# Four down projections of a fused four-layer model as seven products of half blocks in place of eight, with three weight sums on VectorE and one on GpSimd

## The reference, cut to what matters

```python
def swiglu(h, w_gate_up, w_down):
    g, u = jnp.split(h @ w_gate_up, 2, axis=-1)
    return (jax.nn.silu(g) * u) @ w_down

x = x + swiglu(rms_norm(x, ffn_norm[layer]), ffn_w_gate_up[layer], ffn_w_down[layer])
```

## Time and profile before

| | |
|---|---|
| runs of the kernel before | 1708.64, 1708.91, 1709.92 us; median 1708.91 |
| span of the profiled execution | 1710.4 us |
| TensorE busy | 1674.5 us, 98% of the span |
| weight loads busy (beside the matmuls) | 1414.8 us, 83% |
| VectorE, ScalarE, GpSimd busy | 775.4, 318.5, 58.8 us |
| DMA | 289 MB, mean 169 GB/s |

### The profile page before, as it was taken

The page is one execution under the profiler, slowest core; times in us unless marked ns, Lnnn a source line. Parts: engine busy times, 40 slices in busy tenths (PEclk is TensorE's granted clock), DMA queues, the critical chain, the costliest instruction groups (busy, mean ns, idle before and its releaser), DMA issues.

```text
span 1710.4 us, 23078 instructions
## 1 busy us (share of the span) xinstructions
PE 1674.5 (98%) x9352; PEld 1414.8 (83%) x9352; DVE 775.4 (45%) x1677; ACT 318.5 (19%) x700; POOL 58.8 (3%) x84
## 2 busy tenths in 40 slices
PE   8999999999999999999999999999999999999998
PEld 6758888888888867888888785788878898788887
DVE  6545354323365414644345576456643183433300
ACT  3241210000042102100000322322211041222200
POOL 0000000000000000191000000000000000000000
PEclk9999999999999999999999999999999999999999
DMA  6445478865654663666554233244434503444455
GB/s 228 138 136 188 144 242 302 293 234 196 210 166 160 225 227 132 249 217 237 184 162 160 87 123 99 87 137 158 148 119 153 169 6 114 138 156 149 157 162 172
DMA packets 79881, 289.24 MB, mean 169 GB/s; under 512 B 8992, under 2 KB 10016, under 8 KB 79264
## 3 DMA queue, kind: packets, MB, share of 16 engines
q1 hardware_dynamic: 79776, 287.76, 50.0%
HBM read 286.68 MB, written 1.05 MB: 168 GB/s over the span
## 4 chain that ended last, share of the span: by engine, by line
PE 94%; DVE 4%; ACT 1%; issue 1%; DMA 0%; SPq 0%; DVEq 0%; ACTq 0%
PE acc L395 72%; PE acc L464 4%; PE acc L960 3%; PE acc L450 3%; PE acc L405 1%; PE score L925 1%; PE acc L939 1%; PE acc L577 1%; PE score L601 1%; PE score L557 1%; PE acc L900 1%; PE acc L628 1%; PE turned L612 0%; PE score L789 0%; PE stat L431 0%
## 5 line engine op out<-in xcount | busy, mean ns | idle before, releaser
L395 PE MATMUL acc<-H,ring 128*128 128x256 f32 x3520 | 772.6, 381 | 6.9 <-DVE H L1522 3.0
L395 PEld LDWEIGHTS acc<-H,ring 128*128 128x128 f32 x3520 | 667.7, 190 | 108.2 <-issue 12.4
L395 PE MATMUL acc<-FFN,ring 128*128 128x256 f32 x1408 | 304.9, 379 | 0.0
L395 PEld LDWEIGHTS acc<-FFN,ring 128*128 128x128 f32 x1408 | 267.3, 190 | 36.8 <-issue 0.4
L395 PE MATMUL acc<-big,ring 128*128 128x256 f32 x880 | 192.1, 379 | 0.9 <-PE acc L395 0.9
L395 PEld LDWEIGHTS acc<-big,ring 128*128 128x128 f32 x880 | 166.9, 190 | 24.6 <-issue 2.0
L1679 DVE SCALAR_TENSOR_TENSOR bT<-bT,cond 128x1024 f32<-128x1024 f32 x58 | 75.7, 1305 | 80.0 <-DMA bT<-ada_in 76.3
L1874 DVE SCALAR_TENSOR_TENSOR pair<-acc,cols,pair 128x255 f32<-128x255 f32 x84 | 40.5, 483 | 132.8 <-ACT pair L1170 129.7
L1537 DVE TENSOR_TENSOR X<-acc,X 128x256 f32<-128x256 f32 x48 | 20.4, 425 | 148.0 <-PE acc L395 138.9
L1170 ACT ACTIVATE pair<-acc,cols 128x256 f32<-128x256 f32 x84 | 47.2, 564 | 173.6 <-PE acc L395 173.6
L1539 DVE SCALAR_TENSOR_TENSOR X<-acc,mod,X 128x256 f32<-128x256 f32 x24 | 11.6, 484 | 144.6 <-PE acc L395 141.2
(11 more groups left out here) (421 smaller groups left out, 1356.0 us busy)
## 6 DMA issues: line engine op xcount, KB each, us to landing
ring<-stream SPq DMA_DIRECT2D x440, 512.0 KB, 3.5
bT<-ada_in SPq DMA_DIRECT2D x70, 512.0 KB, 4.4
big<-ada_in SPq DMA_DIRECT2D x26, 512.0 KB, 4.5
big<-ssm_in SPq DMA_DIRECT2D x2, 1024.0 KB, 5.7
cols<-cols_in SPq DMA_DIRECT2D x1, 1165.5 KB, 8.5
X<-x_in SPq DMA_DIRECT2D x4, 256.0 KB, 4.6
MEM<-mem_in SPq DMA_DIRECT2D x1, 1024.0 KB, 11.8
y_out<-X SPq DMA_DIRECT2D x8, 128.0 KB, 3.4
```

The source lines that it names most:

```text
L395: mm = nc.tensor.matmul(dst, w[:, k * cols_per:(k + 1) * cols_per], r, start=first and n == 0, stop=last and n == len(src) - 1)
```

## The change

A pair of output tiles (j of 4) by a group c of middle tiles (8, 8 and 6 tiles, so halves of 4, 4 and 3) is a product of 2x2 blocks: two output tiles by two halves of the group for the weights, two halves of the group by two halves of the 256 tokens for the middle. Eight block products become seven by Strassen's rule (in Winograd's form): 128x128 weights by 128 tokens, h of them (h = 4, 4, 3) per block. A group of one pair is a chunk; there are 12 chunks in a down stage and each takes two slots of the stream, laid out anew by `_down_slots`.

- Four of the seven products need sums of weight blocks. `sum_weights` on VectorE makes s1 = a21 + a22, s2 = s1 - a11 and s4 = a12 - s2; `weight_gaps_of` on GpSimd makes a11 - a21. Each has one buffer. So a sum of chunk n+1 waits for the product of chunk n that reads the same buffer (`weight_sums_used`), and TensorE's product waits for the sum (`weight_sums`, `weight_gaps`).
- `sum_mids` on VectorE makes four combinations of middle blocks per group: after k = 8 and k = 16 of the up stage and at its end.
- `combine_upper` and `combine` on VectorE build the two output tiles from the seven sums in two banks, after ScalarE's `corner` has copied one of them out.
- SP loads a slot only after the sums of the chunk that used the buffer are made.
- In up1 the set-up pieces move: `state_decays` from k = 8 to 7, `input_factors` from 11 to 8, `input_product` from 14..19 to 10..15, and six of the eight `drive_powers` into k = 16..21. Two stay in down1.
- `late_lead` replaces `lead` after down0 and down1: the first two lead tiles take rows 0 to 5 first, then rows 6 and 7, and the sum of squares stands behind them.
- The inverse roots after down0 and down1 use ScalarE's Abs_reciprocal_sqrt, and the reciprocal on VectorE goes.

```diff
             def down(name):
-                n = COUNT[name][1]
-                for k in range(n):
-                    bank_free(TILE0[name] + k)
...
-                        product(b[:, 0:S], w, [at(FFN, i) for i in range(lo, hi)], first=c == 0, last=c == 2)\
-                            .then_inc(slot_used, 1)
+                i = int(name[-1])
+                for j in range(4):
+                    t = TILE0[name] + 2 * j
+                    bank_free(t + 1)
+                    a, b = acc[t % 4], acc[(t + 1) % 4]
                     for c in range(3):
...
+                        block_product(a[:, 0:P], w[:, 0:h * P], x[0][0], first=first)
+                        block_product(a[:, 2 * P:3 * P], w[:, h * P:2 * h * P], x[1][0])
+                        if j == 0:
+                            pe.wait_ge(mid_sums, 3 * i + c + 1)
+                        if c < 2:
+                            block_product(b[:, P:2 * P], w2[:, h * P:2 * h * P], d4, first=first).then_inc(slot_used, 2)
+                        for e in sum_order(c):
+                            if c == 2 and e == 0:
+                                block_product(b[:, P:2 * P], w2[:, h * P:2 * h * P], d4, first=first).then_inc(slot_used, 2)
...
+                            if e == 0:
+                                pe.wait_ge(weight_gaps, n + 1)
+                            else:
+                                pe.wait_ge(weight_sums, 3 * n + e)
+                            block_product(dst, summed_weights[e], d, last=last and e in (1, 3)).then_inc(weight_sums_used, 1)
...
+            def weight_gaps_of(name):
+                for n in range(12):
...
+                        pool.wait_ge(weight_sums_used, sum_uses(name, n - 1, 0))
...
+                    g.tensor_tensor(summed_weights[0][:, 0:m], ring[s % RING][:, 0:m], ring[(s + 1) % RING][:, 0:m],
+                                    ALU.subtract).then_inc(weight_gaps, 1)
...
+            def sum_weights(name, n):
...
+                for e, (dst, x, y, op) in enumerate(((s1, a21, a22, ALU.add), (s2, s1, a11, ALU.subtract),
+                                                     (s4, a12, s2, ALU.subtract)), 1):
+                    if n:
+                        dve.wait_ge(weight_sums_used, sum_uses(name, n - 1, e))
+                    v.tensor_tensor(dst, x, y, op).then_inc(weight_sums, 1)
...
+            def paired_residual(name, gain=None, adas_with=0, drive=False, next_gain=None, gained_in=None):
+                begin(name)
+                for j in range(4):
+                    for c in range(3):
+                        if 3 * j + c + 1 < 12:
+                            sum_weights(name, 3 * j + c + 1)
+                        if c and 2 * j + c - 1 < adas_with:
+                            ada(1)
+                    if drive:
+                        if j < 2:
+                            drive_powers(1, 2 + j, H)
+                    if name == "down0" and j == 1:
                         lru_parameters()
...
+                    combine_upper(a, home)
+                    dve.wait_ge(weight_sums_used, 4 * (CHUNK0[name] + 3 * j + 3))
+                    outs_of = combine(a, b, home, score[0])
...
+                sum_weights(f"down{layer + 2}", 0)
+                sum_mids(layer + 2, 2)
                 if s5:
                     local_kernels()
-                residual(f"down{layer + 2}", 3, lambda k: mod_col(layer, 5, k))
+                paired_residual(f"down{layer + 2}", lambda k: mod_col(layer, 5, k))
```

230 lines of the change are left out of this document (184 added, 46 removed).

## The result

The changed kernel takes 1730.31 us (median of 4 runs, 1729.4 to 1730.54), the kernel before 1709.41 beside it (1708.64 to 1712.35): 1.0116 times as long, 95% interval 1.0102 to 1.013. So it is slower, by 20.9 us; forecast were 11.2 us, 1720.1, in a range of 1707 to 1732 that holds the time, near its upper end.

The account below looks back on a forecast made before the run. It took TensorE, busy 1674.5 of 1710.4 us, as the bound. Pace -29.7, waits 9.0 + 10.6 + 3.7, clock 8.7, stage ends 2.5 + 1.4 + 2.3 + 1.8 and up1 0.9 gave +11.2: 1720.1 us, range 1707 to 1732.

Parts of the forecast that it names:

- pace, 2464 at 111.7 ns: Down stages: 2464 matmuls of 128 columns, paced by the weight load, take TensorE from 304.9 to 275.2 us, -29.7.
- wait in down0, chunk 7: down0, second pair: `lru_parameters` (9.4 us) and `ada` stand before s1, due at 9.8 and ready at 18.8; TensorE waits 9.0.
- wait in down2, chunk 1: down2, start: middle sums and `local_kernels` (13.0 us) delay s1 to 20.4 us against 9.8 due; TensorE waits 10.6.
- wait in down1, chunk 4: down1, first pair: `drive_powers` (4.4 us) plus GpSimd and VectorE keeping each other off; wait 3.7 us, without contention 1.0.
- first chunk of down3: down3: VectorE has only sums and combination there, so no wait, 0.
- clock: After TensorE's long waits the clock falls to 1.2 GHz: three falls at 2.9 us, +8.7, bounds 0 and 11.6.
- up1: up1: `state_decays`, then `input_factors` and a middle sum right behind, make TensorE wait 0.9 us once more, +0.9.
- The rival at 108.5: Down stages: matmuls of 128 columns come at the very half, 108.5 ns, 7.9 us less, 1712.2; chance 0.07.
- the rival of showing waits: Down stages: 336 blocks behind semaphores cost 30 to 50 ns each, +10 to +17, 1730 to 1737; chance 0.13.
- The deadline of 9.8 us: Down stages: the second s1 is due 9.8 us behind a pair's end; VectorE's work between two s1 must fit.
- Ends of the stages: Behind each down stage VectorE needs three combining pieces and two tiles, not one: +2.5, +1.4, +2.3, +1.8 for down0 to down3.
- From the profile to the median: Whole kernel: the profiled span of 1710.4 is 1.5 above the median, 1708.91, so 1721.6 becomes 1720.1 us.

Follow-up runs that it names:

- the experiment with halves: The kernel before, with each down matmul of 256 tokens made as two of 128 tokens, eight products and no sums: 1722.96 us, 1.0068 of the kernel before.

## Why the prediction was right, and short

The sum was right in its direction and in what it is made of, and 7 us short in size. The terms, read between the starts of matmuls in the two profiled executions:

| term | forecast | profiles |
|---|---|---|
| pace, 2464 at 111.7 ns | -29.7 | -29.0 |
| wait in down0, chunk 7 | +9.0 | +10.3 |
| wait in down2, chunk 1 | +10.6 | +12.1 |
| wait in down1, chunk 4 | +3.7 | +3.2 |
| first chunk of down3 | 0 | +0.8 |
| clock | +8.7 | +8.5 (11.6 - 3.1) |
| end of down0 | +2.5 | +2.5 |
| end of down1 | +1.4 | +1.2 |
| end of down2 | +2.3 | +2.2 |
| end of down3 | +1.8 | +1.2 |
| up1 | +0.9 | +2.7 |
| start of the first transfer; a wait ahead of line 1055 | - | +0.8, +0.6 |
| sum | +11.2 | +17.1 of 18.3 |

The 1.2 us that are left are slower blocks and short waits inside down0 (0.7) and down1 (0.5).

- **Pace.** Right: 111.7 ns from start to start in the undisturbed blocks. The term is 0.7 us smaller than forecast since the 304.9 us of before are busy time, with the tail of each stage's last matmul; from start to start they are 304.2. And the experiment with halves shows that it is the price of the narrow matmul and not of the new order. The rival at 108.5 falls. So does the rival of showing waits: a block behind a semaphore that was already free started 111 or 112 ns behind the last matmul. Down1 of the kernel with all three pieces spread has 84 blocks, and its 616 matmuls come every 111.8 ns on average. No wait of TensorE for GpSimd's difference appears, as forecast.
- **The deadline of 9.8 us.** Right in place, mechanism and, within 1.5 us, size; spreading each piece removed its wait. The sizes in down0 and down2 were short mainly for one reason: I took VectorE's instructions at their times of before. Beside GpSimd some are longer: in down0 the tiny ones take 10.8 us in place of 9.4 (one took 1.13 us where its neighbours took 0.17). The run without GpSimd's work gives 1.9 of down0's wait and 1.0 of down2's to it (there a sum of middle blocks took 1.52 us and its equal neighbours 0.56). In down2 some 0.6 us more stand ahead of the first memset, which the 13.0 us of the earlier trace rows don't hold. Contention was counted in down1 alone, with 2.7 of 3.7 us; it was 1.9 of 3.3.
- **The clock.** The size was right and the working was not, so that 8.7 meets 8.5 is luck. I took three falls at 2.9 us. There were six, at 1.7 to 2.5. In all profiled executions together, 29 of 45 unfilled waits of 2.8 to 3.9 us (from start to start) had a fall, and the one of the kernel before, ahead of line 880, didn't come in the profiled execution after: line 975's wait of 3.5 us had none. The run with filled waits shows further that the term is no sum of falls.
- **Ends of the stages.** Right within 0.6 us each.
- **up1.** The step that failed: 0.9 forecast, 2.7 measured, and the wait was 3.6 where it had been 0.9. The prediction moved `state_decays` with the length of before and expected the new wait from `input_factors` and a middle sum behind it. (It also puts the wait of before on `state_decays` at k = 7; in the kernel before that piece stands at k = 8.) The order of time shows what happened. GpSimd's piece and VectorE's, one k earlier than before, now run at the same time; GpSimd, then one of four such instructions of VectorE in the changed kernel:

```profile
756.37 5.50 POOL L1553 TENSOR_TENSOR chunk_tab<-chunk_tab 128x512 f32<-128x512 f32 x4
```

```profile
756.60 1.14 DVE L2432 TENSOR_SCALAR small<-small 128x32 f32<-128x32 f32 x1
```

  The kernel before had 0.24 us for each of these four, since its own 6.16 us of such GpSimd work ended at 751.33, before them, and held one instruction for 1.03 us in place of 0.37. So 4 x 0.89 - 0.66 = 2.9 us, about the 2.7. It is contention once more, by arithmetic on two traces; no run here tested it alone, and spreading `state_decays` hid it.
- **down3.** Not "0": the first sums of the stage come 0.8 us late. Without GpSimd's work the stage is 0.6 us shorter.
- **From the profile to the median.** The sum was made on a span of 1710.4 and then lowered by the same 1.5 us. The profiled execution of before had taken 1712.35 us in all, with a granted clock of 0.998; later runs of that kernel with 0.999 took 1708.7 to 1710.9, but for one of 1712.4, and those with 0.998 took 1711.6 to 1713.0. That of after took 1730.54, no more than its median. So of the 10.2 us between 1720.1 and 1730.3, 7.1 are missing in the sum (18.3 against 11.2), and the other 3.1 are this step. The likely reason is the fall at line 880's wait: the profiled execution of before has it, the clocks say that most runs have not, and the sum treated it as part of the kernel on both sides. Only profiled executions show where a clock fell, so this isn't shown.
- **The range.** It holds 1730.3, but by some luck: its part above 1730 was there for the waits that show, a rival that fell.

The forecast's direction was right for its reasons: the long pieces of VectorE, not the pace, made the kernel slower, and with them and up1's set-up spread the same change is worth 15 us.

On contention the prediction cited a rule of the Trainium skill, GPSIMD Engine Reference, Specifications (the SBUF interfaces are shared with VectorE, with contention for VectorE instructions that have two SBUF inputs or run in a 2-port perf mode; the prediction named the first kind only). For that kind the trace agrees (a sum of 0.69 us took 1.64). It also shows tensor-scalar operations held, which have one input (0.97 us in place of 0.35 on 256 columns in down1, and the four of 1.13 in up1). The page's second kind may be these; no run here shows in which mode they ran.

## What to carry to other kernels

When an engine off the critical path gets small periodic work with a deadline, look at its longest uninterrupted piece between two deadlines and not at its busy share: VectorE was busy for 54 of 82 us in down0 and for 54.5 of 70 once the piece was cut, and only the cut mattered. Price the narrower instruction by a row of that width: an eighth less arithmetic was here a tenth less time, since the weight loads set the pace. A sum that comes late can hold the transfers too, where a buffer is freed by it: look for what stands behind those transfers in the queue. And where work moves to GpSimd to relieve VectorE, count what it gives back: of the 31 us taken over, VectorE lost 18 to 22 again, in the instructions that ran beside it.

## What the runs showed of the hardware

- A wait of TensorE of 2.1 us (from start to start, chunk 10 of down0 in the changed kernel with filled waits, 5.6 us behind one of 0.8) was enough for the clock to fall to 0.50, and one of 3.5 us, at line 975, was followed by no fall in one execution and by one of 6.8 us in another; in each of the six unfilled waits of 8.5 us and more it fell while the wait still lasted.
- During waits of 10 and 12 us filled with matmuls that nobody reads the clock stayed at 1.00.
- GpSimd's subtraction beside VectorE's sums holds VectorE's instructions in single cases to 1.64 us (0.69 alone), and tiny ones to 1.13 us (0.17 alone).
- Waits on semaphores that are already free cost TensorE nothing that the profile shows (111.8 ns per matmul over 84 blocks), even when the weight loads have no slack.
- Matmuls of 128x128 float32 weights start 112 ns apart with 128 columns and 216 ns apart with 256.
